# Sample attention of a hybrid decoder step: four head pairs of a request in four column groups, folded per request, pages over two queues

## What is computed

```python
def fox_sample(q, k, v, logf, k_past, v_past, logf_past):
    c_past = jnp.cumsum(logf_past.astype(F32), axis=1)
    c_new = c_past[:, -1:, :] + jnp.cumsum(logf.astype(F32), axis=1)
    cp = c_past.transpose(0, 2, 1)
    cn = c_new.transpose(0, 2, 1)
    s_past = jnp.einsum('bthd,bshd->bhts', q, k_past, preferred_element_type=F32) * scale
    s_past = s_past + (cn[..., :, None] - cp[..., None, :])
    s_new = jnp.einsum('bthd,bshd->bhts', q, k, preferred_element_type=F32) * scale
    s_new = s_new + (cn[..., :, None] - cn[..., None, :])
    s_new = jnp.where(jnp.tril(jnp.ones((T, T), bool)), s_new, -jnp.inf)
    p = jax.nn.softmax(jnp.concatenate([s_past, s_new], -1), axis=-1).astype(v.dtype)
    return (jnp.einsum('bhts,bshd->bthd', p[..., :P], v_past)
            + jnp.einsum('bhts,bshd->bthd', p[..., P:], v))
```

## Time and profile before

| | us |
|---|---|
| three runs: lowest, median, highest | 5233.84, 5237.98, 5239.48 |
| profiled execution, its own time | not shown |
| profiled execution, span from first to last instruction | 5223.1 |
| PE busy in it | 4683.3 |
| DVE, ACT, POOL busy in it | 1092.1, 654.3, 260.1 |

### The profile page before, as it was taken

How to read it: one execution, slowest core, us unless ns; L and a number is a source line. 1 busy time by engine, 2 the same in 40 slices (tenths; PEclk the granted TensorE clock), 3 DMA queues, 4 the chain that set the end, 5 groups by cost and what they waited for, 6 DMA issues and landing times.

```text
span 5223.1 us, 55407 instructions
## 1 busy us (share of the span) xinstructions
PE 4683.3 (90%) x20862; PEld 3164.5 (61%) x20862; DVE 1092.1 (21%) x2491; ACT 654.3 (13%) x1105; POOL 260.1 (5%) x456
## 2 busy tenths in 40 slices
PE   7688888988889999999995879898888999999998
PEld 4477576755445666666654766666653456666665
DVE  2344222133212000000024541312332110000001
ACT  0222011133100000000003220102231000000000
POOL 1000002100000000000010000130000000000000
PEclk8888787989899999999997888798998999999999
DMA  3300101102241111111112001011024211112011
GB/s 75 17 0 0 38 21 23 42 26 65 93 139 33 36 40 36 36 41 34 39 38 5 0 5 41 13 35 42 13 65 157 86 33 36 36 36 58 22 34 61
DMA packets 274079, 215.20 MB, mean 41 GB/s; under 512 B 23696, under 2 KB 236912, under 8 KB 272640
## 3 DMA queue, kind: packets, MB, share of 16 engines
q1 hardware_dynamic: 255296, 163.64, 12.2%
q0 software_dynamic: 18624, 49.50, 3.4%
HBM read 197.55 MB, written 15.53 MB: 41 GB/s over the span
## 4 chain that ended last, share of the span: by engine, by line
PE 82%; DVE 7%; issue 5%; ACT 3%; DMA 3%; DVEq 0%; POOL 0%; ACTq 0%; POOLq 0%; SPq 0%
PE ps L760 79%; PE ps L764 3%; DMA out_rwkv_shift_sample<-big 1%; DVE hT L1379 1%; ACT wd L2136 1%; DMA big<-in_x_prompt 0%; DVE big L1571 0%; DMA wd<-in_state_rwkv 0%; ACT wd L2123 0%; ACT big L2106 0%; DMA out_y_prompt<-big 0%; ACT sil L2152 0%; DVE sil L1372 0%; DVE big L1579 0%; DVE big L1541 0%
## 5 line engine op out<-in xcount | busy, mean ns | idle before, releaser
L760 PE MATMUL ps<-hT,ring 128*128 128x352 f32 x6528 | 1966.1, 463 | 25.6 <-DVE hT L1379 10.7
L760 PEld LDWEIGHTS ps<-hT,ring 128*128 128x128 f32 x6528 | 1246.7, 192 | 738.7 <-issue 29.1
L760 PE MATMUL ps<-big,wd 128*128 128x352 f32 (+3 forms) x2576 | 711.6, 439 | 65.5 <-ACT big L1969 42.3
L760 PEld LDWEIGHTS ps<-big,wd 128*128 128x128 f32 (+2 forms) x2576 | 462.5, 192 | 311.5 <-ACT big L1969 42.6
L1901 DVE TENSOR_TENSOR big<-ps,sil 128x1056 f32 x44 | 55.3, 1258 | 1189.5 <-PE ps L760 1189.5
L760 PE MATMUL ps<-wd 128*128 128x128 f32 (+4 forms) x1560 | 235.0, 297 | 70.0 <-ACT wd L2136 21.7
L760 PE MATMUL ps<-big 128*128 128x128 f32 (+4 forms) x1488 | 244.0, 337 | 52.5 <-POOL big L636 14.8
L760 PEld LDWEIGHTS ps<-wd 128*128 128x128 f32 (+2 forms) x1560 | 207.1, 203 | 136.5 <-issue 76.2
L760 PE MATMUL ps<-ring,hT 128*128 128x128 f32 (+1 forms) x2304 | 261.5, 275 | 0.0
L764 PE MATMUL ps<-ident,big 128*128 128x128 f32 (+4 forms) x998 | 175.4, 322 | 95.4 <-ACT big L1992 28.3
L760 PEld LDWEIGHTS ps<-ring,hT 128*128 128x128 f32 (+1 forms) x2304 | 256.9, 183 | 5.2 <-issue 2.4
(11 more groups left out here) (336 smaller groups left out, 3122.6 us busy)
## 6 DMA issues: line engine op xcount, KB each, us to landing
big<-in_cache_fox_k SPq DMA_DIRECT2D x128, 256.0 KB, 2.9
ring<-in_w_in SPq DMA_DIRECT2D x60, 512.0 KB, 3.8
ring<-in_w_gate SPq DMA_DIRECT2D x44, 512.0 KB, 3.8
ring<-in_w_up SPq DMA_DIRECT2D x44, 512.0 KB, 3.8
wd<-in_w_down SPq DMA_DIRECT2D x16, 1408.0 KB, 7.0
big<-in_cache_fox_v SPq DMA_DIRECT2D x80, 256.0 KB, 4.0
big<-in_cache_fox_v POOLq DMA_DIRECT2D x48, 256.0 KB, 4.3
ring<-in_w_out SPq DMA_DIRECT2D x16, 512.0 KB, 4.1
```

Of the source, the lines that this page charges most:

```text
L760: return pe.matmul(out, lhsT, rhs, start=start, stop=stop, skip_group_check=True)
```

## The change

Head pair p of a request now has partitions 32p to 32p+31, so the rows of a group are ordered by pair, then request, then the 8 rows; the four requests add into the same rows, with queries that are zero in the other requests' columns. The scores of a request are issued when all four of its pairs are copied, one request behind the transposes, in turns over the four column groups, for which `keyt` has eight parts instead of two. In the values the eight pages of a request go in turns to the four column groups of bank 6 or 7, and each request has its own masking and its own fold (`om_b`, `tok4`), added up in bank 5. The transposed probabilities are put back into the order by request when they are copied. The masks are brought into the new order by one matmul with a permuted identity (`by_pair`). The loops over the two groups are written out, so that no copies of the group's part are needed but one, and POOL issues 3 of the 8 key pages of the second group.

```diff
-        keyt = [region((sil, NP * i), NP) for i in range(2)]
+        keyt = [region((sil, NP * i), NP) for i in range(2)] + [region((ringf, NP * i), NP) for i in range(3)] + [hT[:, i, 0:NP] for i in (5, 6, 7)]
...
-        om = pss[:, 0:FW]
+        om_b = [om_a, pss[:, 0:FW]]
+        om_n = pss[:, FW:2 * FW]
...
+        K_SP = lambda g: NPG if g == 0 else V_SP
...
-                        for j in range(NPG):
-                            page = sp.value_load(ptab[0:1, bass.ds(g * (4 * NPG) + (b * NPG + j), 1)], min_val=0, max_val=N_POOL - 1)
+                        for j in range(K_SP(g)):
+                            page = sp.value_load(ptab[0:1, g * (4 * NPG) + b * NPG + j:g * (4 * NPG) + b * NPG + j + 1], min_val=0, max_val=N_POOL - 1)
...
+                    if g:
+                        for b in range(4):
+                            pool.wait_ge(fgr_pe, G_PE.at(it - 1, f"V{b}"))
+                            pool.sem_inc(passed, 1)
+                            for j in range(V_SP, NPG):
...
+                                pool.dma_start(slot[b][:, j, :], I["cache_fox_k"][bass.ds(l, 1), bass.ds(page, 1)].rearrange("a n p h d -> p (a n h d)")).then_inc(vpage_in[b], 16)
...
+                pe.wait_ge(fs_dve, FS_DVE.at(l, "tok4"))
+                mm(ps[:, 7, 0:44], by_pair, row_consts).then_inc(fs_pe, 1)
...
+                    def key_scores(b):
+
+                        pe.wait_ge(*ev(b, 2))
+                        pe.wait_ge(*ev(b, 3))
+                        for a in range(2):
+                            for p in range(4):
+                                mm(ps[NS * p:NS * p + NS, a, :], qb[:, 4 * g + b, p, :], keyt[4 * (b % 2) + p][:, 512 * a:512 * a + 512], False, b == 3)
+                        for p in range(4):
+                            last = mm(ps[NS * p:NS * p + NS, 2, 0:TS], qb[:, 4 * g + b, p, :], kn[:, p, TS * (4 * g + b):TS * (4 * g + b) + TS], False, b == 3)
+                        G_PE.mark(last, fgr_pe, f"S{b}")
...
                     for b in range(4):
-                        pe.wait_ge(page_in[b], it * ((NPG + V_SP) * 16) + NPG * 16)
                         key_tr(b, 0)
-                        for p in range(4):
-                            if p < 3:
-                                key_tr(b, p + 1)
-                            pe.wait_ge(*ev(b, p))
-                            o = slice(NS * b, NS * b + NS)
-                            last_one = p == 3
-                            for a in range(2):
-                                mm(ps[o, a, :], cur_q[:, b, p, :], keyt[p % 2][:, 512 * a:512 * a + 512], False, last_one)
-                            last = mm(ps[o, 2, 0:TS], cur_q[:, b, p, :], cur_k[:, p, TS * b:TS * b + TS], False, last_one)
-                            G_PE.mark(last, fgr_pe, f"S{b}{p}")
+                        key_tr(b, 1)
+                        if b:
+                            key_scores(b - 1)
+                        key_tr(b, 2)
+                        key_tr(b, 3)
+                    key_scores(3)
...
+                        for j in range(NPG):
+                            q = j % 4
+                            last = mm(ps[NS * q:NS * q + NS, 6 + b % 2, :], pts[:, j, NS * b:NS * b + NS], slot[b][:, j, :], j < 4, j >= 4)
+                        G_PE.mark(last, fgr_pe, f"V{b}")
+
+                    def fold(b):
+
+                        pe.wait_ge(*gd(f"om{b}"))
+                        for p in range(4):
+                            last = mm(ps[:, 5, 16 * p + TS * b:16 * p + TS * b + TS], om_b[b % 2][:, P * p:P * p + P], tok4, False, b == 3)
+                        G_PE.mark(last, fgr_pe, f"F{b}")
...
-                            last = mm(ps[o, 7, :], pts[:, j, o], slot[b][:, j, :], False, j == NPG - 1)
-                        G_PE.mark(last, fgr_pe, f"V{b}")
...
                     for b in range(4):
+                        fold(b)
+                        if b < 2:
+                            values(b + 2)
```

More of the change, by code:

```diff
@@ L363, in build @@
         NPARAM = 8
+        NFOXC = 4 * 16
         NCOLS_IN = DEPTH * 16
@@ L497, in _ @@
                 sp.sem_inc(passed, 1)
-                with sp.Fori(0, 2) as g:
+                for g in range(2):
                     it = l * 2 + g
                     for b in range(4):
-                        if b == 3:
+                        if g == 0 and b == 3:
                             sp.wait_ge(fp_act, FP_ACT.at(l * 2 + 1, "1oT"))
@@ L1255, in _ @@
                 last.then_inc(fs_pe, 1)
-                with pe.Fori(0, 2) as g:
+                for g in range(2):
                     it = l * 2 + g
@@ L1267, in _ @@
                     G_PE.mark(last, fgr_pe, "bias")
+                    k_sp = l * SP_PAGES + 16 * (K_SP(0) if g == 0 else K_SP(0) + V_SP + K_SP(1))
+                    k_pool = l * POOL_PAGES + 16 * 2 * (NPG - V_SP)
                     def key_tr(b, p):
+                        if p == 0:
+                            pe.wait_ge(page_in[b], k_sp)
+                            if g:
+                                pe.wait_ge(vpage_in[b], k_pool)
                         if b or p >= 2:
                             pe.wait_ge(*(ev(b, p - 2) if p >= 2 else ev(b - 1, p + 2)))
+                        elif g and p == 1:
+                            pe.wait_ge(fgr_dve, G_DVE.at(it - 1, "o"))
                         for j in range(NPG):
@@ L1828, in _ @@
                 on((fp_act, FP_ACT.at(l * 2 + 1, "1oT")))
+                fsm_(v.tensor_copy(by_pair.rearrange("k (p b c) -> k p b c", p=4, b=4), ident[:, :].rearrange("k (b p c) -> k p b c", p=4, b=4)), "perm")
+                on((fox_const, l * NFOXC + NFOXC))
+                v.sem_inc(passed, 1)
+                fsm_(v.tensor_reduce(tok4, row_consts[:, 20:36].rearrange("r (b t) -> r t b", t=TS), AX.X, ALU.add), "tok4")
+                on((fs_pe, l * 2 + 1))
+                v.sem_inc(passed, 1)
+                fsm_(v.tensor_copy(pair_consts, ps[:, 7, 0:44]), "pairs")
                 fsm_(v.memset(qb, 0.0), "qz")
@@ L1841, in _ @@
                 fsm_(v.tensor_tensor_scan(ncs[R64], ones[R64, 0:1].to_broadcast((DB * FH, NP + TS)), lfs[R64], 0.0, ALU.mult, ALU.subtract), "ncs")
-                on(fsd("ncs"), (fox_const, l * 64 + 64))
-                v.sem_inc(passed, 1)
-                with v.Fori(0, 2) as g:
+                on(fsd("ncs"))
+                for g in range(2):
                     it = l * 2 + g
@@ L2138, in _ @@
                         fm(a.copy(hT[:, bass.ds(pp * 2 + u, 1), 0:T].rearrange("p a t -> p (a t)"), ps[:, 4:6, :].rearrange("p a b -> p (a b)")), f"{u}oT")
-                with a.Fori(0, 2) as g:
+                for g in range(2):
                     it = l * 2 + g
@@ L2149, in _ @@
                             on(gp(f"T{b}{p}"))
-                            if b or p == 2:
-                                on(gp(f"S{b}0") if p == 2 else gp(f"S{b - 1}2"))
-                            gm(a.copy(keyt[0], ps[:, 3:5, :].rearrange("p a b -> p (a b)")), f"kt{b}{p}")
+                            if b >= 2:
+                                on(gp(f"S{b - 2}"))
+                            gm(a.copy(keyt[4 * (b % 2) + p], ps[:, 3:5, :].rearrange("p a b -> p (a b)")), f"kt{b}{p}")
                     on(gd("neg"))
```

110 lines of the change are left out of this document (61 added, 49 removed).

## The result

The changed kernel takes 5111.84 us, median of four runs (5105.77 to 5116.83), beside 5235.91 us for the kernel before: ratio 0.9761, 95% interval 0.975 to 0.9773. The forecast was 5122 us. The profiled execution took 5116.24 us with a span of 5114.7 us, so only 1.5 us lie around a span.

A forecast was written before the change was run, and what follows sets the result against it. TensorE (PE) was taken as the path; preparation +2.9, keys and scores -18.8 and -19.6, values -11.2 and -10.8, group start -0.6 gave -58.1 us per layer, -116 in two: 5238 - 116 = 5122 us (66%), range 5098 to 5178.

The forecast's parts named there:

- Four column groups side by side: Long passes of a request's scores and values: four run at once, 0.455 us a round including a surcharge.
- 2.3 us once per request: Key stage: a request's four rounds of scores (1.82 us), small passes and change of form, formerly four times 1.9 to 2.0.
- The rival of two passes at a time: Scores and values: only two passes overlap, eight rounds of 0.43 us; 54 us more in all, 5176 us; chance 10%.
- The ring: Key stage, through VectorE: transposes 0.86, scores 2.3, transposes 0.86 and 0.86, copy 1.66; 6.5 us a request.
- the start of group 0: Key stage, low clock, no scores between: second request's pair 1 begins 8.6 us after the first transposes.
- the tail: End of a group's key stage: transposes and scores 4.9, copy 1.7, scores 2.2, 0.25 us to the softmax.
- the sum: Sample attention: all gains and losses together, -58.1 us per layer, -116 us in two layers.
- Values: Value stage of each group: 18.0 us against 29.2 and 28.8, gains of 11.2 and 10.8 us.
- Preparation: Before the first bias: about 9.9 us instead of 7.0, 2.9 more per layer, between 1.9 and 4.
- Pages: Loads of keys and values, group 1: five on SP, three on POOL, slack 4 to 6 us, no cost.
- the rival of late pages: POOL's queue adds nothing to SP's 205 GB/s: group 1's pages late, 38 us in two layers, 5160 us; chance 12%.
- The clock: Value stages: rises 6.9 us after the start as before; rival that it stays low, 30 us, 5152 us, chance 9%.

The follow-up runs named there:

- the second profile: The changed kernel run once more with nothing changed: 5098.82 us, ratio 0.9749 to the kernel before.

## Why the prediction was right, and where its sizes were off

*Four column groups side by side*: right, and better than taken. I had read a surcharge of 0.025 us a round off three bands of 352 columns; four groups of 512 have none (0.43 us). The term "2.3 us once per request" is 1.89. The rival of two passes at a time would have given 3.6 us of scores; it is refuted for the order written here, and half true for another (4.54 us in the kernel that goes pair by pair).

*The ring*: right in every link. 6.2 us against 6.5; the scores alone are 0.41 shorter than taken, and the rest of the ring is 0.07 longer. Also mis-sized were the start of group 0 (the second request's pair 1 comes 7.3 us after the first transposes, not 8.6) and the tail (8.3, not 9.05). With two rings at 0.3 less these make 2.7 us, about what the keys of group 0 gained beyond the sum (2.5). The terms of the two groups add up to 30.65 and 28.95 us and were put down as 30.5 and 28.8. In group 1 a term is missing: the bias took 2.02 us at a granted clock of 1.00, where it took 3.43 before.

*Values*: 18.0 us were 16.3 in the first group. A request takes 1.86 instead of 2.0 for the reason above, and the clock was back up at the first fold (1.0 us, where I had 1.9 at the low level). DVE's products lie under other work and the folds cost PE 1.0 us each, both as said, and the idle time ahead of the bias of group 1 fell from 1.39 to 0.44 us, 0.95 for the 0.6 of the sum.

*Preparation*: the step is right, the price was too high. Sixteen copies of half the size took 2.20 us, near the lower bound, not 3.4 to 3.7. From the tables' arrival to the bias it is 8.6 us against my 9.9 and 7.0 before; the rest of the +2.4 of the first layer is a later arrival.

*Pages*: nearly no wait, and that with luck. The prediction had a slack of 4 to 6 us and named a wait of PE for DMA in group 1 as a sign of being wrong; the slack is 0.1 to 2.6 us, and the second profile has such a wait, of 0.7 us. The working had the first request's keys complete 10 us after the start of the value stage, but its own terms (first issue at 5.4, a slot of 7.0) allow 12.4 at the earliest; they came at 16.7, and a page took 5.2 us from issue to landing, not 2.9, with the engines full. That the keys were wanted 2 us later than taken, and a page cost SP 1.18 us and not 1.28, left the margin that there is. The roof was too low as well: I took 300 GB/s from a stretch in which the engines were 89% busy at 281; they went to 389. That the second queue carries this change was the argument against the rival of late pages, and the kernel without it shows what it was worth: up to 29.6 us, where I had priced 38.

*The sum*: -116 us were -136.5 in the stretches; 124 by the medians of the first comparison and 132.5 of the second, the remainder being how the rest of the program happened to run, as far as the profiles tell. So it is in part luck that 5122 us came so near the first median: the sum was 20 us too small in the stretches, and 12 of them were lost outside. 5122 us was 10 above the first median, 23 above the second (5098.82), and in the second case at the low end of the range. One statement was plainly wrong: that 15 us lie around the span. It is 1.5; the profiled execution of before had simply been a fast one. Since the sum was taken from the median, nothing came of it.

*The clock* was the largest thing left out. I let it rise in each value stage as before, and in the changed kernel it did, but in six value stages of three experiments it rose later and the stage took 18.7 to 19.1 us. And I did not see that a stage of 16 us at a low clock for its first 6 offers 11 us in all (four times 2.7) to whoever keeps PE busy.

## What to carry to other kernels

Small outputs of 32 columns that share one stationary size can be issued in turns over the four column groups at the full rate of each, if the moving data and the masking permit it; write the turns out in the program, since six passes in a row in one group held the others back here, and four did not. When PE work shrinks this much, look at the same time at the queue that feeds it (here one queue's issue would have taken back 23 to 29 us, and with two queues the pages land 0.1 to 2.6 us before they are needed) and at the idle stretches ahead of each short stage, because what is saved can be lost there to the lower clock.

## What the runs showed of the hardware that was not expected

- Four column groups run at the full rate of one: 16 passes of 512 columns in 1.86 us, with starts 10 to 20 ns apart.
- Passes are held back by a column group with six in a row, not by one with four (0.89 us from pair to pair, and no delay in the values).
- Two queues together reach 361 GB/s for 24 us and 389 for 4, with each page issue on SP at 1.18 us (222 GB/s alone).
- Matmuls that nobody reads pay for themselves: ten passes, 4.56 us while PE would have waited for the softmax, gave back 2.7 us in each value stage and 0.9 in each softmax. In two of the three kernels with such matmuls a shorter low stretch of clock turned up at the next stage (3 to 7 us at the start of group 1 in the first of them), so the gain is read from the sum of the stretches.
